# Ten slots instead of eight for cache pages, and every value page issued by SyncE

## The reference, cut to what matters

```python
# per sequence: 16 pages of 128 keys, 8 heads x 64; 8 blocks of 2 pages
kmean = mean of the keys of each block
gate = einsum('bhqd,bhnd->bhqn', q, kmean);  _, idx = top_k(gate, 3)
sel_k, sel_v = pool_k[page_table[...idx...]], pool_v[...]
s_sel = q . sel_k * scale - slope * distance
s_own = q . own_k * scale - slope * distance      # the 8 new keys
p = softmax([s_sel, s_own]);  out = p_sel @ sel_v + p_own @ own_v
```

## Time and profile before

| | us |
|---|---|
| median of 3 runs (904.36 to 908.85) | 904.87 |
| the profiled execution, its own time | 908.24 |
| its span in the trace | 906.4 |
| TensorE busy | 846.1 (93%) |
| VectorE, ScalarE, GpSimd busy | 455.9, 351.0, 267.7 |
| bytes moved | 197.44 MB, 218 GB/s on average |

### The profile page before, as it was taken

How to read it: one execution, slowest core, us unless ns; L and a number is a source line. 1 busy time by engine, 2 the same in 40 slices (tenths; PEclk the granted TensorE clock), 3 DMA queues, 4 the chain that set the end, 5 groups by cost and what they waited for, 6 DMA issues and landing times.

```text
span 906.4 us, 17053 instructions
## 1 busy us (share of the span) xinstructions
PE 846.1 (93%) x6754; PEld 746.7 (82%) x6754; DVE 455.9 (50%) x708; ACT 351.0 (39%) x502; POOL 267.7 (30%) x326
## 2 busy tenths in 40 slices
PE   5699999999999999999987789879999999999997
PEld 3498998988799989988764556537899999999996
DVE  1444333433233466844686776744864444444353
ACT  2323243232222367355443324173573333432230
POOL 2020000000010131999999999800300000000130
PEclk9599999999899999999999899998999999999998
DMA  9967777879955553416998999998525444644421
GB/s 301 353 202 228 255 242 223 263 226 309 331 174 195 168 159 119 163 47 195 346 314 269 365 329 380 348 348 277 170 72 153 149 139 142 198 141 130 161 70 59
DMA packets 182129, 197.44 MB, mean 218 GB/s; under 512 B 11907, under 2 KB 163705, under 8 KB 182053
## 3 DMA queue, kind: packets, MB, share of 16 engines
q1 hardware_dynamic: 175149, 190.04, 64.8%
q10 hardware_dynamic: 6624, 6.33, 2.2%
q0 software_dynamic: 288, 0.14, 0.1%
HBM read 193.67 MB, written 3.17 MB: 217 GB/s over the span
## 4 chain that ended last, share of the span: by engine, by line
PE 76%; DVE 8%; SPq 5%; DMA 5%; ACT 4%; issue 3%; POOL 1%; DVEq 0%; ACTq 0%; POOLq 0%
PE bank L1599 19%; PE bank L1600 18%; PE bank L1601 18%; PE bank L1871 5%; PE bank L1575 3%; SPq L446 3%; PE bank L1896 2%; DMA raw<-in_w_ada 2%; PE bank L1564 1%; DVE wlo L1089 1%; DMA raw<-in_ffn_wg 1%; DVE kT L1371 1%; PE bank L1631 1%; DMA raw<-in_ffn_wu 1%; PE bank L1625 1%
## 5 line engine op out<-in xcount | busy, mean ns | idle before, releaser
L1089 DVE TENSOR_TENSOR wlo<-raw,whi 128x2048 fp32r<-128x2048 f32 (+1 forms) x80 | 183.3, 2292 | 241.9 <-ACT whi L711 241.6
L1599 PE MATMUL bank<-mh,whi 128*128 128x320 f32 x816 | 257.5, 316 | 0.0
L1601 PE MATMUL bank<-mh,wlo 128*128 128x320 f32 x816 | 252.2, 309 | 0.0
L1600 PE MATMUL bank<-ml,whi 128*128 128x320 f32 x816 | 252.2, 309 | 0.0
L711 ACT CAST whi<-raw 128x2048 fp32r<-128x2048 f32 (+1 forms) x80 | 149.0, 1862 | 232.2 <-PE bank L1601 155.2
L1599 PEld LDWEIGHTS bank<-mh,whi 128*128 128x128 f32 x816 | 153.4, 188 | 10.4 <-issue 10.3
L1600 PEld LDWEIGHTS bank<-ml,whi 128*128 128x128 f32 x816 | 153.5, 188 | 0.1
L1601 PEld LDWEIGHTS bank<-mh,wlo 128*128 128x128 f32 x816 | 153.3, 188 | 0.0
L1599 PE MATMUL bank<-hh,whi 128*128 128x320 f32 x352 | 111.3, 316 | 0.0
L1600 PE MATMUL bank<-hl,whi 128*128 128x320 f32 x352 | 109.6, 311 | 0.0
L1601 PE MATMUL bank<-hh,wlo 128*128 128x320 f32 x352 | 109.5, 311 | 0.0
(11 more groups left out here) (270 smaller groups left out, 1142.1 us busy)
## 6 DMA issues: line engine op xcount, KB each, us to landing
araw<-in_w_ada SPq DMA_DIRECT2D x28, 1024.0 KB, 5.2
raw<-in_ffn_wg SPq DMA_DIRECT2D x22, 1024.0 KB, 7.1
raw<-in_ffn_wu SPq DMA_DIRECT2D x22, 1024.0 KB, 7.3
raw<-in_ffn_wd SPq DMA_DIRECT2D x16, 1024.0 KB, 5.5
raw<-in_cache_k SPq DMA_DIRECT2D x64, 256.0 KB, 4.4
raw<-in_cache_v SPq DMA_DIRECT2D x60, 256.0 KB, 5.4
raw<-in_w_in SPq DMA_DIRECT2D x10, 1024.0 KB, 5.2
raw<-in_w_ada SPq DMA_DIRECT2D x8, 1024.0 KB, 12.2
```

The lines of the kernel that those rows point to most:

```text
L1089: dve.tensor_tensor(wl(slot_w(phase, u))[:, 0:size], landed(phase, u)[:, 0:size], wh(slot_w(phase, u))[:, 0:size].bitcast(F32), ALU.subtra ...
L1599: pe.matmul(bank[:, b, 0:T], wh(slot)[:, c], h_, start=(start and n == 0), stop=False)
L1600: pe.matmul(bank[:, b, 0:T], wh(slot)[:, c], l_, start=False, stop=False)
L1601: ins = pe.matmul(bank[:, b, 0:T], wl(slot)[:, c], h_, start=False, stop=(stop and n == len(parts) - 1))
```

## The change

- `KV_RING` is 10. Slot 8 is `kvm`, memory shared with the start of `mh` (the modulated input of W_in, later of W_out). Slot 9 is `kvu`, shared with the start of `uT`, which holds the projected queries, keys and values. The last 14 pages follow a list, `KV_LAST`.
- In `uT` the places of k and v are exchanged, so that slot 9 covers q and most of v, and k stays.
- Page 9, the first in slot 9, waits for the prompt's scores, the turned tokens and the spread queries; page 8 waits for the end of W_in.
- All four DMAs of every value page are issued by SyncE; ScalarE issues none and reads no page numbers.
- W_out's units 0 and 1 wait for pair 3's last two keys (the last users of slots 6 and 7), units 2 and 3 for `v_used` 27 and 28.
- ScalarE waits for `v_used` 25 (page 56, in slot 8) before it writes convolution chunks to `mh`.
- The prompt's convolution rows are stored after page 14; the samples' still after page 32.

```diff
-KVN, KV_RING = 64, 8
+KVN, KV_RING = 64, 10
+KV_LAST = (0, 1, 2, 3, 4, 5, 8, 9, 0, 1, 4, 5, 2, 3)
...
-    return kvi % KV_RING if kvi < KVN - 8 else (0, 1, 2, 3, 4, 5, 2, 3)[kvi - KVN + 8]
+    return kvi % KV_RING if kvi < KVN - len(KV_LAST) else KV_LAST[kvi - KVN + len(KV_LAST)]
...
+        with ExitStack() as scope:
+            kvm = sb("kvm", [P, UMAX], F32, scope)
         mh = sb("mh", [P, NCH, T], F32R)
...
+        with ExitStack() as scope:
+            kvu = sb("kvu", [P, UMAX], F32, scope)
         with ExitStack() as scope:
             uT = sb("uT", [P, 12, T], F32, scope)
...
             k = kv_slot(kvi)
+            if k >= 8:
+                return (kvm, kvu)[k - 8][:, :]
...
-                else:
-                    sp.wait_ge(w_used, WIN[0] + (7, 7, 10, 9)[kvi - RING])
-                load_pages(sp, cache, kvi, numbers[8 * (k % 4 // 2) + k % 2:], range(3 if cache == "v" and j < 3 else 4))
-                if kvi == KV_RING + 3:
+                elif kvi < 9:
+                    sp.wait_ge(w_used, WIN[0] + (7, 7, 10, 9, 10)[kvi - RING])
+                else:
+                    sp.wait_ge(ps_mm, NH)
+                    sp.wait_ge(tok_t, 8)
+                    sp.wait_ge(q_ready, 1)
+                load_pages(cache, kvi, numbers[8 * (k % 4 // 2) + k % 2:])
+                if kvi == KV_RING + 4:
...
-                        sp.wait_ge(v_used, 16 + 7 + u)
+                        sp.wait_ge(kt_ready, 2 * (24 + 7 + u))
...
-                load(WOUT, u, cols(i["w_out"], slice(UC * u, UC * u + UC)), NCH * UC, (v_used, 24 + u - 1))
+                load(WOUT, u, cols(i["w_out"], slice(UC * u, UC * u + UC)), NCH * UC, (v_used, 24 + u + 1))
...
-                def last_page(k, page):
-
-                    kvi = values_at(j - 1, k)
-                    act.wait_ge(kt_ready, 2 * (8 * j + k + 1))
-                    load_pages(act, "v", kvi, page[8 * (k % 4 // 2) + k % 2:], range(3, 4))
...
-                    if j and k:
-                        last_page(k - 1, numbers)
...
+                act.wait_ge(v_used, 24 + 1)
                 act.mul(mh[:, NCC + c, :], tmp[:, c, :], par2[:, 16 + c:17 + c]).then_inc(mh_ready, 1)
```

More of the change, by code:

```diff
@@ L429, in ada_count, with page_numbers, load_pages @@
             return 8 * (a - ADA0 - a % 2) + 16
-        def page_numbers(b, engine=mybir.EngineType.SP):
+        def page_numbers(b):
             _, page = nc.values_load_multi_w_load_instructions(
-                pages[0:1, NPG * b:NPG * b + NPG], engines=[engine], min_val=0, max_val=NPOOL - 1,
+                pages[0:1, NPG * b:NPG * b + NPG], engines=[mybir.EngineType.SP], min_val=0, max_val=NPOOL - 1,
                 skip_runtime_bounds_check_because="a page table holds indices into the pool, as the reference reads it")
             return page
[L438 to L444, removed]
-                else:
-                    eng.dma_start(slot[x:P:4, :].rearrange("p (h f) -> p h f", h=NH),
-                                  src.rearrange("a h (g r) d -> g (a h) (r d)", r=4)).then_inc(kv_in[kv_slot(kvi)], 16)
         @block.sync
         def _(sp):
+            def load_pages(cache, kvi, page):
+                slot = kv_raw(kvi)
+                for x in range(4):
+                    src = i["cache_" + cache][0][bass.ds(page[2 * x], 1)]
+                    if cache == "k":
+                        sp.dma_start(slot[:, 512 * x:512 * x + 512], src.rearrange("a h (g r) d -> (a h g) (r d)", r=8)).then_inc(kv_in[kv_slot(kvi)], 16)
+                    else:
+                        sp.dma_start(slot[x:P:4, :].rearrange("p (h f) -> p h f", h=NH),
+                                      src.rearrange("a h (g r) d -> g (a h) (r d)", r=4)).then_inc(kv_in[kv_slot(kvi)], 16)
             sp.dma_start(con[:, 0:C_LN], i["consts"][:, 0:C_LN]).then_inc(ld_ident, 16)
@@ L561, in _ @@
                     sp.wait_ge(w_lo, WIN[0] + WIN[2] - RING + kvi + 1)
-                else:
-                    sp.wait_ge(w_used, WIN[0] + (7, 7, 10, 9)[kvi - RING])
-                load_pages(sp, cache, kvi, numbers[8 * (k % 4 // 2) + k % 2:], range(3 if cache == "v" and j < 3 else 4))
-                if kvi == KV_RING + 3:
+                elif kvi < 9:
+                    sp.wait_ge(w_used, WIN[0] + (7, 7, 10, 9, 10)[kvi - RING])
+                else:
+                    sp.wait_ge(ps_mm, NH)
[3 more added lines that the diff above has]
+                if kvi == KV_RING + 4:
                     sp.wait_ge(gl_out, 1)
                     sp.dma_start(o["conv_prompt_new"][0, 0], cout).then_inc(stored_early, 16)
-                if kvi == 4 * KV_RING:
+                if kvi == 32:
                     store_conv()
@@ L921, in _ @@
                     elif c < 12:
-                        act.copy(uT[:, c, :], src).then_inc(u_out, 1)
+                        act.copy(uT[:, c + 4 if c < 8 else c - 4, :], src).then_inc(u_out, 1)
                     if head_done(slot - 1) in (1, 3, 5, 7):
@@ L963, in keys_low @@
             def keys_low(j, between={}):
-                def last_page(k, page):
-                    kvi = values_at(j - 1, k)
-                    act.wait_ge(kt_ready, 2 * (8 * j + k + 1))
-                    load_pages(act, "v", kvi, page[8 * (k % 4 // 2) + k % 2:], range(3, 4))
-                numbers = None
                 for k in range(8):
                     n = 8 * j + k
-                    if j and k % 4 == 1:
-                        numbers = page_numbers(2 * (j - 1) + k // 4, mybir.EngineType.Activation)
                     act.wait_ge(kt_ready, 2 * n + 1)
@@ L983, in keys_low @@
                         act.copy(kT_view(k, 1), bank_keys(1)).then_inc(kt_high, 1)
-                    if j and k:
-                        last_page(k - 1, numbers)
                     if k in between:
                         between[k]()
-                if j:
-                    last_page(7, numbers)
             def probs(j):
@@ L1775, in turn_tokens @@
             def turn_tokens(e):
-                at = (8, 4)[e % 2] + 2 * (e // 2)
+                at = (4, 8)[e % 2] + 2 * (e // 2)
                 pe.wait_ge(u_out, (2, 6, 8, 12)[e])
@@ L1810, in prompt_qk @@
                     pe.wait_ge(ps_ready, h)
-                q, k = uT[r, h // 2, :], uT[r, 4 + h // 2, :]
+                q, k = uT[r, h // 2, :], uT[r, 8 + h // 2, :]
                 pe.matmul(bank[:, 6, 0:P], q[:, 0:P], k[:, 0:P], start=True, stop=True)
@@ L1904, in own_scores @@
                         ins = pe.matmul(bank[QG * g4:QG * g4 + QG, 6, NS * b2:NS * b2 + NS], qo[:, 2 * j + b2, g4, :],
-                                        uT[:, NHP + g4, SEQ:T], start=True, stop=True)
+                                        uT[:, 8 + g4, SEQ:T], start=True, stop=True)
                 ins.then_inc(own_ready, 1)
```

## The result

The changed kernel is slower, by 0.5 to 0.7%. Measured in alternation with the kernel before it had a median of 913.54 us (910.91 to 915.14, 5 runs) against 907.43 us, ratio 1.0068 with a 95% interval of 1.0044 to 1.0093. A second series (10 runs against 27) gave 1.0051, 1.0028 to 1.0073. The profiled execution after took 910.91 us, the lowest of its five, with a span of 908.9 us.

What follows compares the result with a forecast made beforehand. Bound: the landing of pages 60 and 61, forecast 4.0 us earlier. TensorE wins 5.6 us, or 3.8 if its clock falls; the middle, 4.8, off the 904.87 us median gives 900.1 us, range 897.8 to 904.8.

Steps and rivals of the forecast that it cites:

- The place: Fourth pair's values in the attention stage: only the landing of pages 60 and 61 is on the path, 5.6 us of waits.
- the edits priced at nothing: Convolution-chunk wait, new slots' waits, k and v exchange, W_out's slot waits: nothing, the first at most 0.5 us if late.
- the chain of ScalarE and VectorE behind W_out: After W_out unit 0 lands: earlier cast, SiLUs bound to VectorE's multiplies, unit 1's remainder ready 1.1 us earlier, at 614.6 us.
- the sum of 90.2 us: SyncE's queue after 489.45 us: issues, number readings and stores total 90.2 us, reaching page 56 at 579.6, before 582.39.
- The head start of two pages: SyncE's resumption at 489 us: ten slots put two key pages ahead, 5.5 us of DMA time.
- The second step: From page 56 on: backlog used up, so pages 60 and 61 land at 605.7 and 608.7 us, 4.0 us earlier.
- Rival (c): SyncE at page 56: 12.6 us of added issue not absorbed, page 56 at 591.0, end 5.9 us later, 910.8; chance 0.08.
- rival (a): SyncE becomes the bound at 0.84 us a value issue: page 60 lands at 608.7, gain 1.5 us, 903.4; chance 0.17.
- rival (b): TensorE's clock falls at pages 60 and 61 as before: gain 3 us, 901.9; chance 0.68 together with the forecast.
- Rival (d): VectorE's remainder of W_out comes 2.4 us earlier, ScalarE's table load no longer behind the cast: 6.5 us, 898.4; chance 0.07.
- The prediction's signs of being wrong: Page 56 issued after 583 us, page 61 landing at 612 or later, or TensorE moved before 600 us.
- One sign of being right: The DMA share of 582 to 600 us falls below 1.10.

Runs made afterwards that it cites:

- x8: Changed kernel, but ScalarE issues the fourth transfer of pairs 0 to 2's value pages and W_out's units 0 and 1 follow page 55; 903.67 us, 0.9956 of before.
- x5: Changed kernel, but ScalarE issues the fourth transfer of pair 0's eight value pages; 912.85 us, 1.0044 of the kernel before.
- x6: Changed kernel, but ScalarE issues the fourth transfer of pair 2's value pages (48 to 55); 906.72 us, 0.9994 of the kernel before.
- x3: Kernel before with its eight slots, but SyncE issues all four transfers of every value page; 919.36 us, 1.0110 of the kernel before.
- x2: Changed kernel with its ten slots, but ScalarE issues the fourth transfer of pairs 0 to 2's value pages; 906.71 us, 0.9990 of the kernel before.

## Why the prediction was wrong

**What held.** The place was right: the landing of pages 60 and 61 decides. So was the resumption at 489 us with page 26, the cost of one issue (0.602 us at least, 3.95 us for eight key transfers), the edits priced at nothing (no wait for `v_used` 25, for the new slots' first use or for W_out's slots shows up in the trace after), and the chain of ScalarE and VectorE behind W_out, which x8 laid open: cast at once, SiLUs bound to VectorE's products, then the remainder of unit 1 as the next wait, 1.4 us where 0.2 to 2 were put.

**The step that failed** is the sum of 90.2 us, "so it reaches page 56 at 579.6 us". It added minimum durations over the whole stretch from 489 to 580 us and took everything by which SyncE's issues had been stretched before as "slack to take". The same minima for the kernel before, with three issues a value page and eight key pages, sum to 81.7 us; it took 92.9. So the prediction let 11.2 us vanish. In the changed kernel 5.4 of them stayed. Phase by phase, readings of page numbers included:

| SyncE's phase, us | before | the prediction's terms | after |
|---|---|---|---|
| keys 2 (8 pages, then 6) | 18.7 | 13.1 | 14.5 |
| values 1, with the stores | 27.7 | 30.3 | 32.2 |
| keys 3 | 20.7 | 18.2 | 19.2 |
| values 2 | 24.7 | 27.4 | 28.5 |
| to page 56 | 1.2 | 1.2 | 1.2 |
| sum | 92.9 | 90.2 | 95.6 |

Every phase ran over its minimum, by 1.0 to 1.9 us. The excess is largely in single issues that took long; here is the longest into slot 9 (1329 ns) beside the median (602 ns):

```profile
L455 SPq DMA_DIRECT2D kvu<-in_cache_v x16: 602/602/1329, 465.5 to 590.7; - x16
```

The prediction ascribed such stretching to a full queue. No run shows that cause: the issue of 1329 ns belongs to page 39, whose last transfer landed 3.2 us behind it, while page 47's keys, with 9.1 us to their last landing, went out at the usual 333 ns each. What stretches single issues stays open.

Of the 12.6 us moved behind the wait at 489, 8.3 came back as longer value phases (32.2 - 27.7 and 28.5 - 24.7); two key pages fewer and a shorter keys 3 returned 5.7. x5 and x6 show the same from the other side: eight issues taken off before the wait don't count, the same eight taken off in the last value phase count in full.

What that does to the data is read from the landings, the last transfer of a page in us from the first key transposition, as means of the three traces of before and the four of after:

| page | before | after | difference |
|---|---|---|---|
| 31 (last of keys 2) | 88.9 | 83.3 | -5.6 |
| 39 (last of values 1) | 114.5 | 112.6 | -1.9 |
| 47 (last of keys 3) | 137.6 | 137.0 | -0.6 |
| 55 (last of values 2) | 161.0 | 161.5 | +0.5 |
| 59 | 173.0 | 175.7 | +2.7 |
| 60 | 182.1 | 186.1 | +4.0 |

The head start of two pages was there, 5.6 us where the prediction had 5.5. Values 1 spent 3.7 us of it, and from page 56 on the changed kernel fell behind. Three stretches show how; of the trace before (columns as in the earlier trace rows):

```profile
512.00:536.00 24.00, 22.96 (x244) 16.69 (x247) 15.38 (x16) 6.71 (x6) 23.06 (x33) 0.88 0.98 316
546.00:584.00 38.00, 33.58 (x406) 23.67 (x402) 25.02 (x43) 14.74 (x20) 36.58 (x50) 0.97 1.08 365
584.00:604.00 20.00, 16.79 (x230) 9.75 (x226) 9.04 (x25) 9.45 (x19) 2.82 (x4) 1.00 1.10 348
```

and of the trace after:

```profile
512.00:536.00 24.00, 21.19 (x261) 15.05 (x259) 17.93 (x21) 6.72 (x6) 23.06 (x34) 1.00 0.90 286
546.00:584.00 38.00, 34.02 (x398) 24.02 (x398) 26.56 (x49) 12.36 (x17) 36.67 (x50) 0.96 1.07 364
584.00:604.00 20.00, 16.50 (x198) 9.94 (x198) 7.68 (x15) 9.41 (x18) 3.98 (x5) 0.91 0.96 305
```

In a key phase SyncE needs 2.3 us a page with the numbers and the DMA engines 2.7, so a backlog builds up; in a value phase of the changed kernel it is the other way round, 3.4 against 3.0, and the backlog shrinks. In values 1 there was little of it, and the DMA engines moved 286 GB/s instead of 316. What keys 3 had piled up kept them full until 584 us, 364 GB/s, as before. Then it was used up, and they moved 305 GB/s instead of 348 until 604 us: 0.86 MB less, by estimate 2.5 us at 348 GB/s, and page 60 began 2.7 us later in this trace.

**The second step** that failed followed from "the backlog is used up at page 56". That it was used up there is right, but the prediction made a gain of it: it put 24.9 us between page 56's issue and page 60's products. It is 27.2 to 28.4 us in all the traces of before and after. SyncE issued pages 56 to 59 in 12.8 us, as expected (12.5), a page each 3.2 us or 329 GB/s; the DMA engines moved less than that, and the prediction had them keep up. Why they fell behind was not tried. W_out's unit 0 landed 8.4 us after its issue (the cast in the trace after began at 606.49 us, the issue was at 598.07), where the sum had 5.8 with its wait behind page 59. x8, without W_out in between, has page 60 landed 22.2 us behind page 56's issue. Had only this step failed, page 60 would have begun at 608.0 us (580.8 + 27.2), 1.7 us earlier than before; had only the first, at 610.2 us (585.25 + 24.9), 0.4 us later. Together they make the 612.46 us of the trace.

**The rivals.** Rival (c) had the direction and the place: page 56 went out at 585.25 us, on the point from which it was said to decide (582.0 to 586.8 us in the four traces). It was given 0.08, although the prediction itself had 3.13 + 0.3 us of issue against 3.0 of transfer. That comparison by phase should have been the forecast, not a remark under rival (a). Its price, a loss of 5.9 us, came near the measured one, but that was luck: it let none of the 12.6 us be absorbed and put page 56 at 591.0 us, too late, and then page 60 only 24.6 us behind it, too early. Rival (a) had the bound right and its size wrong: 16 value issues took 13.38 us in the trace after, 0.836 each, as it supposed, but it kept a gain because it too had page 60 25.5 us behind page 56. The slow products of rival (b) came, 1.94 us for the 16 products of page 60 and of page 61; in x8, with no idle before them, 32 took 1.93. Rival (d) does not hold: in x8, where the cast was out of the way, ScalarE's table load still began only behind VectorE's product:

```profile
603.73 1.28 ACT L1061 ACT_TABLE_LOAD   x1 [1.86 <-DVE yT L1477]
```

**The signs.** The prediction's signs of being wrong appeared: page 56 after 583 us, page 61's products not before 615.49. One sign of being right came as well and told nothing: the DMA share from 582 to 600 us fell, to 0.97, because the DMA engines were fed less, not because the work was done earlier.

The Trainium skill's sentence weighed there ("DMA: Bandwidth & Descriptors", "Issuing engines are not separate DMA queues") calls the issue time usually small beside the transfer; x3 measured 1.1% of the kernel for it. The prediction's 357 GB/s "with both" include the last key pages; from 566 to 582 us, where both engines issued value pages, the kernel before moved 348, as with SyncE alone.

**Still open**: the ratios, 1.0068 and 1.0051, are 4.6 to 6 us and the seven traced executions show 3.5. The difference is within the spread of single executions (903 to 913 us before, 908 to 917 after), and no trace shows a second place.

## What to carry to other kernels

Compare the issuing engine and the DMA engines phase by phase, and follow the backlog between them: what a fast phase has piled up helps the next phase only until it is used up, and a sum of the issuer's minima does not show when that is. Durations above the minimum are not time that can be filled with more work; here about half of them stayed. An issue is only worth moving off a queue where that queue is the bound until the next long wait; before a wait it is free. Here the deeper ring paid (x8, 0.9956, against x2, 0.9990) once what then held the last transfers, W_out's two loads among the pages, was moved into the wait that it leaves.

## What the runs showed of the hardware

Two kinds of transfer of 256 KiB occupy the issuing engine for quite different times: a key page's (128 partitions, pieces of 2 KiB) 0.333 us, a value page's (32 partitions, pieces of 1 KiB) 0.602 us, on SyncE as on ScalarE (0.61). The DMA engines move the first kind at 382 and the second at 348 GB/s, so the second kind costs 81% more in issuing and 10% more in moving. Whether the number of pieces or of partitions sets this was not tried.
